# Encoder layer on one core: order of the first loads, token tile 0 before the norm-row copy, and eleven identity products at the head

## What is computed

```python
def rmsnorm(x, g):
    xf = x.astype(jnp.float32)
    y = xf * lax.rsqrt(jnp.mean(xf * xf, axis=-1, keepdims=True) + EPS)
    return (y * g.astype(jnp.float32)).astype(x.dtype)

h = rmsnorm(x, norm1[l])
proj = h @ w_in[l]
q, k, v, p = ...
att = diff_attention(q, k, v, rel_table, lam, subln_g[l], lam_init)
pool = pool_mixer(p, w_pool[l], pool_scale[l])
x = x + jnp.concatenate([att, pool], axis=-1) @ w_out[l]
x = x + moe(rmsnorm(x, norm2[l]), ...)
return rmsnorm(x, final_norm)
```

## Time and profile before

| what | value |
|---|---|
| median of 3 runs | 2193.36 us (2190.24 to 2193.45) |
| profiled execution, its own time | 2195.68 us |
| span in its trace | 2193.9 us |
| mean granted TensorE clock | 0.987 |
| PE busy | 2130.5 us, 97% of the span, 10256 instructions |
| DVE / ACT / POOL busy | 672.6 / 617.5 / 507.7 us |
| DMA | 500.73 MB, mean 228 GB/s |

### The profile page before, as it was taken

One profiled execution on the slowest core, in us unless ns is written; L12 is line 12 of the kernel. 1 busy time (PEld: TensorE's weight loads), 2 busy tenths in 40 slices (PEclk: granted clock), 3 DMA queues, 4 the chain that ended last, 5 costly groups with the idle time before them and its releaser, 6 DMA issues.

```text
span 2193.9 us, 30475 instructions
## 1 busy us (share of the span) xinstructions
PE 2130.5 (97%) x10256; PEld 1003.7 (46%) x10257; DVE 672.6 (31%) x1909; ACT 617.5 (28%) x1202; POOL 507.7 (23%) x521
## 2 busy tenths in 40 slices
PE   8999999996999999999998999999999999999997
PEld 6547676443444444344343434434443444444443
DVE  3322997345121222212222221222112211222223
ACT  2000887113222232212232222222222222222223
POOL 3181121123212221121122122221212121222223
PEclk9999999997999999999999999999999999999998
DMA  8001100426768778578869686785889868677775
GB/s 304 12 36 45 73 1 1 163 95 231 258 208 313 263 265 311 198 258 324 331 189 387 235 313 246 242 295 178 328 314 366 326 246 289 240 257 268 254 274 192
DMA packets 151899, 500.73 MB, mean 228 GB/s; under 512 B 10681, under 2 KB 36046, under 8 KB 151310
## 3 DMA queue, kind: packets, MB, share of 16 engines
q1 hardware_dynamic: 116192, 444.81, 52.9%
q0 software_dynamic: 33792, 50.35, 11.1%
q10 hardware_dynamic: 1874, 5.02, 0.6%
HBM read 461.26 MB, written 43.09 MB: 230 GB/s over the span
## 4 chain that ended last, share of the span: by engine, by line
PE 95%; DMA 3%; POOL 1%; issue 1%; DVE 0%; ACT 0%; ACTq 0%; SPq 0%; DVEq 0%; POOLq 0%
PE psum L1755 42%; PE psum L1790 15%; PE psum L1443 7%; PE psum L1553 5%; PE psum L1801 5%; PE psum L1576 3%; PE psum L1542 3%; PE psum L1439 2%; PE psum L1742 2%; PE psum L1681 2%; DMA weights<-in_w_down 2%; PE psum L1763 2%; PE psum L1825 1%; PE psum L1813 1%; PE psum L1585 1%; DMA weights<-in_w_up 1%
## 5 line engine op out<-in xcount | busy, mean ns | idle before, releaser
L1755 PE MATMUL psum<-weights,work 128*128 128x512 f32 (+2 forms) x3008 | 951.2, 596 | 3.1 <-DMA weights<-in_w_up 3.1
L1755 PEld LDWEIGHTS psum<-weights,work 128*128 128x128 f32 (+2 forms) x3008 | 366.9, 159 | 519.3 <-issue 517.9
L730 POOL DMA_INDIRECT residual_rows<-work x184 | 286.8, 1559 | 532.4 <-ACT work L955 482.0
L1790 PE MATMUL psum<-weights,work 128*128 128x512 f32 x768 | 337.5, 592 | 0.0
L1252 DVE SCALAR_TENSOR_TENSOR work<-psum,work 128x4 f32<-128x4 f32 x47 | 7.6, 163 | 841.0 <-PE psum L1674 841.0
L686 POOL DMA_INDIRECT work<-normed_rows,work x48 | 54.6, 1137 | 750.4 <-PE psum L1681 578.6
L1790 PEld LDWEIGHTS psum<-weights,work 128*128 128x128 f32 x768 | 142.2, 190 | 160.7 <-issue 160.7
L925 ACT ACTIVATE work<-psum 128x256 f32<-128x256 f32 x188 | 72.0, 383 | 418.1 <-PE psum L1755 391.6
L1319 DVE TENSOR_SCALAR work<-psum 128x256 f32<-128x256 f32 x188 | 79.8, 424 | 290.2 <-ACT work L925 289.9
L955 ACT ACTIVATE work<-psum,work 128x256 f32<-128x256 f32 x184 | 72.2, 475 | 321.8 <-PE psum L1790 229.5
L905 ACT ACTIVATE work<-psum 128x512 f32<-128x512 f32 x96 | 57.6, 600 | 342.7 <-PE psum L1681 342.2
(11 more groups left out here) (237 smaller groups left out, 1858.1 us busy)
## 6 DMA issues: line engine op xcount, KB each, us to landing
weights<-in_w_gate SPq DMA_DIRECT2D x64, 2048.0 KB
weights<-in_w_up SPq DMA_DIRECT2D x64, 2048.0 KB
weights<-in_w_down SPq DMA_DIRECT2D x64, 2048.0 KB, 11.3
residual_rows<-x SPq DMA_DIRECT2D x9, 512.0 KB, 3.9
normed_rows<-work ACTq DMA_DIRECT2D x9, 512.0 KB, 4.0
x<-in_x SPq DMA_DIRECT2D x8, 512.0 KB, 9.1
weights<-in_w_in SPq DMA_DIRECT2D x16, 256.0 KB, 8.8
weights<-in_w_in SPq DMA_DIRECT2D x8, 512.0 KB, 11.7
```

The source lines that it names most:

```text
L730: pl.indirect_dma_start(acc_d[:, :], bass.IndirectOffsetOnAxis(dest[:, b:b + 1], 0), yrow[:, b * BLK:(b + 1) * BLK], None, compute_op=ALU. ...
L1755: mm = pe.matmul(out.rearrange("p (m n) -> p m n", m=2), xT[:, k, lo:lo + cols], wgu[:, :, k, blk * BLK:(blk + 1) * BLK], start=(k == 0), ...
L1790: mm = pe.matmul(bank(4 + h), actT[:, k, :], wdn[:, k, h * HALF:(h + 1) * HALF], start=False, stop=(k == DT - 1))
```

## The change

On SP two token tiles are loaded first, then four blocks of weights, token tile 2, four more blocks, token tile 3. The totals stay the same, and so does all that follows.

On DVE the scaling of token tile 0 comes first, then the copy of the gains, then the scaling of tile 1. `subg` is made after the four `move_hT`. The gains now go through bank 3 instead of bank 0, so the wait for their copy moves from the transposes of tile 0 to those of tile 1.

On PE eleven 128x128 products of the identity with itself, whose result nobody reads (bank 7), stand ahead of the wait for `grows`. Tile 2 is transposed after all of tile 0's products, and tile 3 after all of tile 1's.

```diff
-            for i in range(4):
+            for i in range(2):
                 sp.dma_start(xv[:, i, :], xd[i]).then_inc(s_rows[i], 16)
-            for k in range(DT):
-                sp.dma_start(w_pc[:, k, :], wd[k][:, 3 * HALF:]).then_inc(s_w[k], 16)
+            for i in range(2, 4):
+                for k in (4 * i - 8, 4 * i - 7, 4 * i - 6, 4 * i - 5):
+                    sp.dma_start(w_pc[:, k, :], wd[k][:, 3 * HALF:]).then_inc(s_w[k], 16)
+                sp.dma_start(xv[:, i, :], xd[i]).then_inc(s_rows[i], 16)
...
-            dve.wait_ge(s_gps, 1)
-            dve.tensor_copy(gains[:, 0:21], bank(0, 21)).then_inc(s_gains, 1)
-            dve.wait_ge(s_gains, 1)
-            dve.tensor_scalar(subg[:, :], gains[:, 20:21], 1.0 - LAM_INIT, None, ALU.mult).then_inc(s_gains, 1)
...
             scale_tokens(0)
+            dve.wait_ge(s_gps, 1)
+            dve.tensor_copy(gains[:, 0:21], bank(3, 21)).then_inc(s_gains, 1)
             scale_tokens(1)
+            dve.wait_ge(s_gains, 1)
             for i in range(4):
                 move_hT(i)
+            dve.tensor_scalar(subg[:, :], gains[:, 20:21], 1.0 - LAM_INIT, None, ALU.mult).then_inc(s_gains, 1)
...
+            def keep_clock(b, n):
+
+                for _ in range(n):
+                    pe.matmul(bank(b, P), ident[:, :], ident[:, :], start=True, stop=True)
+
             pe.wait_ge(s_const, 4)
+            keep_clock(7, 11)
             pe.wait_ge(s_grows, 64)
-            pe.transpose(bank(0, 21), grows, ident[0:21, 0:21]).then_inc(s_gps, 1)
+            pe.transpose(bank(3, 21), grows, ident[0:21, 0:21]).then_inc(s_gps, 1)
...
-                if i == 0:
+                if i == 1:
                     pe.wait_ge(s_gains, 1)
...
-                    if i < 2 and k == 3:
+                    if i < 2 and k == DT - 1:
                         transposes(i + 2)
```

## The result

| | before | changed |
|---|---|---|
| median | 2193.31 us | 2197.09 us |
| runs, spread | 22, 2190.24 to 2196.51 | 22, 2193.87 to 2200.32 |
| profiled execution's span | 2193.9 us | 2195.5 us |

The ratio is 1.0017, 95% interval 1.0011 to 1.0022: 3.8 us slower, clear of noise, and on the whole within the 0.2% that the forecast called no change (a little of the interval lies beyond). The forecast was 2196.3, or +2.9 us.

What follows compares the result with a forecast made beforehand. PE was taken to bound the kernel (95% of the chain). +1.2 us for the wait less work moved ahead of it and +1.7 for the clock gave +2.9, from 2193.36 to 2196.3 us; range 2190.7 to 2198.8.

Steps and rivals of the forecast that it cites:

- The loads: SP queue in the head: tile 3 lands at 15.2 instead of 9.11 us, tile 2 transposed at 17.6 instead of 14.58.
- What PE does meanwhile: PE in the head: tile 0's products end near 13.9 us, then PE waits 3.7 us until 17.6.
- From there on: PE from 17.6 us at 2.4 GHz: 12.45 us of work until the wide products at 30.05, +1.2 us taken.
- The clock: PE behind the 3.7 us wait: 3.4 us at 1.2 GHz, half of it lost, +1.7 us.
- the clock holds: Rival, PE behind the wait: clock stays up, only +1.2 us, 2194.6 us; chance 0.15.
- The signs: In the head: tile 3's squares about 15 us, tile 2's scaling 16.4, PE idle 3 to 4, wide products from about 31.5.
- signs of being wrong: In the head: tile 3 landing by 12 us, no PE wait over 2 us, or wide products before 28.7.
- A fall of the clock between the identity products and tile 0's products: PE between 6.45 and 9.7 us: tile 0's products at 0.214 each would end near 16.6; sum unchanged.
- Identity products and tile 0 first: Start of the head on PE: 1.05 + 1.92 + 0.86 = 3.8 us gain at most, all lost in the later wait.
- Faster loads: Rival, DMA in the head: mixed order ends the slow stretch, tile 3 lands at 13.4, 2192.9 us; chance 0.20.
- The clock staying low over all the work behind the wait: Rival, PE over 12.45 us of work: up to 5.0 us lost, sum +6.2, 2199.6 us; chance 0.08.
- Tile 3 not late: Rival, SP queue: tile 3's load not held up by those ahead, 3.8 us gain at most, 2189.5 us; chance 0.07.

Runs made afterwards that it cites:

- Loads alone: Kernel before with only the new order of loads, tile 2's transposes still after k=3: median 2197.74 against 2192.98 us, ratio 1.0021.
- the reordered ACT: Changed kernel, but ACT scales tile 2 before it squares tile 3: median 2192.64 against 2194.20 us before, ratio 0.9995.
- second profile: Profile of the changed kernel timed once more without edits: median 2197.37 against 2194.20 us before, ratio 1.0014.
- identity products alone: Kernel before plus only the eleven identity products ahead of the wait for the norm rows: median 2193.15 against 2194.48 us, ratio 0.9994.
- identity products and tile 0 first: Changed kernel with the old order of loads and place of the transposes (after k=3): medians 2191.31 and 2190.99 us, ratio 0.9991 twice.

## Why the prediction was right

*The loads.* Right as a mechanism: tile 3 last, ACT's squares of it ahead of tile 2's scaling, PE waiting for that. Loads alone and the reordered ACT show both halves. The size of the term was off: tile 3 was to land at 15.2 and did so at 15.9 (16.6 in the second profile), so tile 2's transposes came at 18.16 instead of 17.6. The lower rate in the slow stretch, 250 GB/s instead of 278 for 4.5 us, is 0.13 MB, some 0.3 us at 409 GB/s, and explains at most half. Without the identity products the rate was 275 and tile 3 still came at 16.1; the rest stays open.

*What PE does meanwhile.* The wait was 2.8 us and not 3.7: tile 0's products ended at 15.4 instead of 13.9, because they waited for the weights, w block 7 above all: the instructions that need it began at 14.67, where the prediction had it landed at 13.5. By the prediction's own rate it would have been 15.2 - 0.52 / 0.394 = 13.9. An error without a price, since it is all ahead of the wait.

*From there on.* +1.2 was forecast for the head at full clock, the first profile gives +2.02. Of the 0.8 between them 0.56 are the later start of tile 2's transposes, and 0.22 that these took 1.09 us and not 0.87.

*The clock.* +1.7 was forecast as a certainty of the forecast's case. It measured 1.64 (changed, second time, and without identity products), 1.4 (loads alone, where the low stretch began in the wait, as the prediction had allowed for), and was nothing in the changed kernel's first profile with the same wait of 2.78 us. So "the clock holds" was not a rival to the forecast but its other outcome: of four profiles with that wait three show the fall. How often it falls in the executions without a profile isn't shown. With tile 3 landing as in the first profile, 2.0 and 3.7 are the head's two outcomes, and in the second profile it lost 4.35; the median's +3.8 (2.4 to 4.8 by its interval) fits executions most of which have the fall. The sum of +2.9 lies within that interval although its first term was 0.8 too small. It took the fall for every execution, which is too much wherever the clock holds; the two errors lean against each other, and that much of the closeness is luck.

*The signs.* Squares of tile 3 at 15.92 (about 15 forecast), tile 2's scaling at 17.07 (16.4), a wait of 2.78 us (3 to 4), wide products at 30.7 and 33.0 (31.5). None of the signs of being wrong appeared. A fall of the clock between the identity products and tile 0's products, which the prediction had weighed, didn't come: the sixteen instructions from 9.88 on took 2.05 us, where at 0.214 each they would have taken 3.4.

*Identity products and tile 0 first.* Right that both are lost in the wait; the bound of 3.8 us for them was too generous by far. With the old loads they bring 1.0 to 1.3, because other loads bind next: the q and k weights, landed at 27.26, in the kernel with identity products alone, and w block 0, landed at 10.4 to 10.7, where tile 0 is scaled first as well. The prediction didn't look for those two.

*The rivals.* Faster loads: no, 250 GB/s in the slow stretch, and 219 to 275 in the other six profiles with this order, where the profiles with the old order have 277 to 294. The mixed order doesn't do away with the slow stretch; if anything it is slower. The clock staying low over all the work behind the wait: in no profile. Tile 3 not late: no.

## What to carry to other kernels

When a load is moved back in a queue, look for the engine whose program touches it before something that is already there: here 3 us hung on one square that stood ahead of a scaling. Give filler work on PE a look at what it speeds up, since a faster head is worth only what the next landing allows. And when instructions are added ahead of large loops, read the row of instruction loads before anything else.

## What was not expected of the hardware

24 more PE instructions ahead of the experts' loops cost 63 us in the changed kernel (2260.79 against 2197.37) and 66 us in the one with identity products and tile 0 first (2257.17 against 2190.99). The instructions stood at two different places. There were 85 and 87 instruction packets instead of 25, and waits of PE of up to 6.8 us for which the profile shows no releaser. In both profiles the waits stand at the gate and up products of the experts (L1752 and L1765, and L1747 and L1760).

A wait of PE of 2.78 us (2.77 with the loads alone) was followed by some 3.4 us at 1.2 GHz in three of four profiles and by none in the fourth, the changed kernel's first. The fall came half a microsecond ahead of the wait's end in one of them (loads alone) and 0.4 us behind it in another (the changed kernel's second). What decides it stays open here.
